# Unequal column parts of 280 and 296 in the dense blocks of a hybrid decoder step, laid side by side over a PSUM bank border

## What is computed

```python
def swiglu(x, w_gu, w_down):
    g, u = jnp.split(x @ w_gu, 2, axis=-1)
    return (jax.nn.silu(g) * u) @ w_down

def trunk_layer(x, ...):
    h = x + 0.5 * swiglu(rms_norm(x, w['g_ffn1']), w['w_ffn1_gu'], w['w_ffn1_down'])
    u = rms_norm(h, w['g_mix'])
    q, k, v, zg, r, us5 = jnp.split(u @ w['w_in'], SPLIT_POINTS, axis=-1)
    ...
    h = h + mix.astype(x.dtype) @ w['w_out']
    h = h + cross_attend(rms_norm(h, w['g_cross']), mem_k, mem_v, w['w_cq'], w['w_co'])
    h = h + 0.5 * swiglu(rms_norm(h, w['g_ffn2']), w['w_ffn2_gu'], w['w_ffn2_down'])
    return h, s_gla, s5_re, s5_im
```

## Time and profile before

| what | value |
|---|---|
| median of three runs | 1283.65 us (1283.48 to 1283.89) |
| profiled execution, its own time | 1281.76 us |
| its span in the profile | 1280.0 us |
| PE busy | 1261.9 us (99% of the span), 10151 matmuls |
| PEld busy | 1218.5 us (95%), 10151 weight loads |
| DVE busy | 856.9 us (67%) |
| ACT busy | 530.4 us (41%) |
| POOL busy | 354.3 us (28%) |
| granted PE clock, mean | 0.996 of full speed |

### The profile page before, as it was taken

How to read it: one execution, slowest core, us unless ns; L and a number is a source line. 1 busy time by engine, 2 the same in 40 slices (tenths; PEclk the granted TensorE clock), 3 DMA queues, 4 the chain that set the end, 5 groups by cost and what they waited for, 6 DMA issues and landing times.

```text
span 1280.0 us, 24086 instructions
## 1 busy us (share of the span) xinstructions
PE 1261.9 (99%) x10151; PEld 1218.5 (95%) x10151; DVE 856.9 (67%) x1061; ACT 530.4 (41%) x803; POOL 354.3 (28%) x411
## 2 busy tenths in 40 slices
PE   7999999999999999999999999999999999999998
PEld 6999999999999999999899997599999999999997
DVE  4986479847985636558565437479995589637953
ACT  6543145511224422574443324246553255414543
POOL 0026623388893201000002100032330133102321
PEclk9999999999999999999999999999999999999998
DMA  6223223263223432125333656322332323323321
GB/s 193 83 83 100 83 84 99 83 136 91 78 66 89 93 79 66 51 69 155 118 91 91 234 199 222 121 83 66 100 100 83 99 83 100 92 82 91 87 63 75
DMA packets 221084, 129.94 MB, mean 102 GB/s; under 512 B 22256, under 2 KB 213280, under 8 KB 220960
## 3 DMA queue, kind: packets, MB, share of 16 engines
q1 hardware_dynamic: 217024, 123.83, 33.1%
q10 hardware_dynamic: 3952, 4.58, 1.1%
HBM read 121.42 MB, written 5.78 MB: 99 GB/s over the span
## 4 chain that ended last, share of the span: by engine, by line
PE 91%; DVE 5%; ACT 2%; issue 1%; DMA 1%; SPq 0%; DVEq 0%; ACTq 0%
PE PS L738 87%; PE PS L1363 1%; DMA AR<-in_x_prompt 1%; DVE xl L2141 1%; DVE ARr L2136 0%; PE PS L808 0%; ACT wh L1502 0%; ACT gua L1651 0%; DVE Hs L2454 0%; PE PS L1449 0%; DVE PS L2120 0%; DVE PS L2130 0%; DVE PS L2123 0%; PE PS L1340 0%; DVE AR L2782 0%
## 5 line engine op out<-in xcount | busy, mean ns | idle before, releaser
L1502 ACT ACTIVATE wh<-raw 128x1024 fp32r<-128x1024 f32 (+1 forms) x126 | 130.1, 1032 | 374.1 <-PE PS L738 374.1
L738 PE MATMUL PS<-yh,wh 128*128 128x288 f32 x960 | 206.1, 296 | 0.0
L738 PE MATMUL PS<-yh,wl 128*128 128x288 f32 x960 | 205.0, 295 | 0.0
L738 PE MATMUL PS<-yl,wh 128*128 128x288 f32 x960 | 205.0, 295 | 0.0
L2029 DVE TENSOR_TENSOR wl<-raw,wh 128x1024 fp32r<-128x1024 f32 (+1 forms) x126 | 154.9, 1229 | 62.3 <-ACT wh L1502 60.9
L738 PE MATMUL PS<-xh,ARr 128*128 128x288 f32 x792 | 173.0, 295 | 0.5 <-ACT sq L1585 0.4
L738 PE MATMUL PS<-xh,wh 128*128 128x288 f32 x736 | 164.2, 305 | 0.1
L738 PE MATMUL PS<-xh,wl 128*128 128x288 f32 x736 | 157.9, 296 | 0.0
L738 PE MATMUL PS<-xl,wh 128*128 128x288 f32 x736 | 157.6, 296 | 0.0
L738 PEld LDWEIGHTS PS<-yh,wh 128*128 128x128 f32 x960 | 154.1, 188 | 1.7 <-DVE yl L2707 0.8
L738 PEld LDWEIGHTS PS<-yl,wh 128*128 128x128 f32 x960 | 154.3, 188 | 0.0
(11 more groups left out here) (378 smaller groups left out, 2206.2 us busy)
## 6 DMA issues: line engine op xcount, KB each, us to landing
raw<-in_w_ffn_gu SPq DMA_DIRECT2D x88, 512.0 KB, 3.7
raw<-in_w_ffn_down SPq DMA_DIRECT2D x32, 512.0 KB, 3.8
raw<-in_w_in SPq DMA_DIRECT2D x16, 512.0 KB, 3.8
raw<-in_w_ckv SPq DMA_DIRECT2D x16, 512.0 KB, 3.7
raw<-in_w_ffn_down SPq DMA_DIRECT2D x16, 384.0 KB, 3.3
Hs<-in_cache_mem_k SPq DMA_DIRECT2D x6, 1024.0 KB, 6.5
raw<-in_w_out SPq DMA_DIRECT2D x8, 512.0 KB, 4.0
raw<-in_w_cq SPq DMA_DIRECT2D x8, 512.0 KB, 4.4
```

The lines of the kernel that those rows point to most:

```text
L738: return e.matmul(out, lhsT, rhs, start=start, stop=stop, **kw)
L1502: e.activation(wh[:, n % 2, 0:K * P], raw[:, n % 4, 0:K * P], ACT.Copy).then_inc(w_hi, 1)
```

## The change

The 576 columns of a dense block are cut at column 280 (`TA`) instead of 288. The first part, 280 columns, goes to the end of the first bank (columns 232 to 511), the second part, 296 columns, to the beginning of the next (columns 0 to 295). The two parts then lie side by side in PSUM, and the eviction reads them as one stretch of 576 columns, `tokens(b)`, where it read two rows of 288. Its other operands lose the `two()`. Each dense matmul pair keeps its weights, its place in the order and its number; the sum of its columns is 576 as before. `mix_part` gets the same parts. The memory key blocks keep their single part of 256 columns. The `unit` products, their halves of 288 columns and their evictions (`halves` at L2208, `two` at L2170) stay, and so does `gate_rank` with L2432. No instruction is added, removed or moved on any engine; 2544 pairs of matmuls and the evictions have other shapes.

The diff, without the evictions at L2393, L2532, L2643 and L2752, which change as L2097 and L2247 do:

```diff
@@ constants @@
 TH = T // 2
+TA = 280
@@ PE, dense @@
-            def dense(n, par, K, xa, xb, width=TH, parts=2, ready=None, inside=None, each=None, ahead=False):
+            PARTS = ((0, TA, 512 - TA), (TA, T, 512))
+            MEMORY = ((0, M, 0),)
+
+            def dense(n, par, K, xa, xb, parts=PARTS, ready=None, inside=None, each=None, ahead=False):
...
                     for wi, (w, x) in enumerate(((wh, xa), (wh, xb), (wl, xa))):
-                        for j in range(parts):
-                            last = mm(bank(b0 + j, width), w[:, par, k * P:(k + 1) * P],
-                                      x[:, k, j * width:(j + 1) * width],
+                        for t0, t1, at in parts:
+                            last = mm(bank(b0, t1 - t0, at=at), w[:, par, k * P:(k + 1) * P], x[:, k, t0:t1],
                                       start=(i == 0 and wi == 0), stop=(i == K - 1 and wi == 2))
@@ PE, memory keys @@
-                    dense(n0 + i, i % 2, KD, mh, ml, width=M, parts=1, ready=(S("memx_lo"), 0) if i == 0 else None)
+                    dense(n0 + i, i % 2, KD, mh, ml, parts=MEMORY, ready=(S("memx_lo"), 0) if i == 0 else None)
@@ PE, mix_part @@
-                        for j in range(2):
-                            last = mm(bank(2 * b + j, TH), w[:, b, k * P:(k + 1) * P], x[:, k, j * TH:(j + 1) * TH],
+                        for t0, t1, at in PARTS:
+                            last = mm(bank(2 * b, t1 - t0, at=at), w[:, b, k * P:(k + 1) * P], x[:, k, t0:t1],
                                       start=(i == 0 and wi == 0), stop=(i == KD - 1 and wi == 2))
@@ DVE @@
+            def tokens(b):
+                return bank(b, T, at=512 - TA)
+
             def halves(b):
                 return PS[:, b:b + 2, 0:TH]
...
-                    STT(two(hk), halves(2 * par), 0.5 if g["half"] else 1.0, two(hk), ALU.mult, ALU.add).then_inc(ps_free, 1)
+                    STT(hk, tokens(2 * par), 0.5 if g["half"] else 1.0, hk, ALU.mult, ALU.add).then_inc(ps_free, 1)
...
-                    TTT(two(gs[:]), halves(6 if n == 2 else 0), two(R[:]), ALU.mult).then_inc(g_scaled, 1)
+                    TTT(gs[:], tokens(6 if n == 2 else 0), R[:], ALU.mult).then_inc(g_scaled, 1)
...
-                    TTT(two(us[:]), halves(2), two(R[:]), ALU.mult).then_inc(ps_free, 1)
+                    TTT(us[:], tokens(2), R[:], ALU.mult).then_inc(ps_free, 1)
...
-                    STT(two(h[:, b, :]), halves(2 * (b % 2)), 0.5, two(h[:, b, :]), ALU.mult, ALU.add).then_inc(ps_free, 1)
+                    STT(h[:, b, :], tokens(2 * (b % 2)), 0.5, h[:, b, :], ALU.mult, ALU.add).then_inc(ps_free, 1)
```

More of the change, by code:

```diff
@@ L2392, in body @@
                     f = i * 2 + (f0 + par)
-                    TTT(two(chunk(PR, f)), halves(2 * par), two(R[:]), ALU.mult).then_inc(ps_free, 1)
+                    TTT(chunk(PR, f), tokens(2 * par), R[:], ALU.mult).then_inc(ps_free, 1)
                 return body
@@ L2531, in _ @@
                 e.wait_ge(mm_done, seq(n) + 3)
-                TTT(two(PR[:, b, :]), halves(2 * (b % 2)), two(R[:]), ALU.mult).then_inc(ps_free, 1)
+                TTT(PR[:, b, :], tokens(2 * (b % 2)), R[:], ALU.mult).then_inc(ps_free, 1)
                 if b:
@@ L2632, in _ @@
                     e.wait_ge(ps_free, seq(n) + 2)
-                STT(two(h[:, i, :]), halves(2 * (n % 2)), 1.0, two(h[:, i, :]), ALU.mult, ALU.add).then_inc(ps_free, 1)
+                STT(h[:, i, :], tokens(2 * (n % 2)), 1.0, h[:, i, :], ALU.mult, ALU.add).then_inc(ps_free, 1)
                 conv(n + 2)
@@ L2751, in _ @@
                 e.wait_ge(mm_done, seq(n) + 3)
-                STT(two(h[:, k, :]), halves(2 * (k % 2)), 1.0, two(h[:, k, :]), ALU.mult, ALU.add).then_inc(ps_free, 1)
+                STT(h[:, k, :], tokens(2 * (k % 2)), 1.0, h[:, k, :], ALU.mult, ALU.add).then_inc(ps_free, 1)
                 conv(n + 2)
```

## The result

The change makes the kernel faster: 1273.32 us (median of 4 runs, 1273.04 to 1275.46) against 1283.77 us for the kernel before beside it. The ratio is 0.9918 with a 95% interval of 0.9906 to 0.9930, so 10.5 us or 0.8%. The profiled execution took 1273.04 us with a span of 1271.2 us; that of the kernel before took 1281.76 and 1280.0.

A forecast was written before the change was run, and what follows sets the result against it. PE's distances between matmuls were taken as the bound. The dense matmuls' -11.0 us, other terms 0, took 1281.76 to 1270.8 us profiled; the median lies 1.9 us above, so 1272.7 us, range 1263 to 1298 us.

The forecast's parts named there:

- What bounds the kernel: PE bounds the kernel: busy 1261.9 of 1280.0 us, 91% of the chain; time is the distances between matmuls.
- The evictions at nothing: 110 DVE evictions read one stretch instead of two rows: at most 1.0 us saved, hidden by the next block; term 0.
- The dense matmuls at 130.9 ns, 11.0 us in all: Dense blocks on PE: 4704 matmuls fall from 133.3 to 130.9 ns, 384 cheap ones lose 0.9 ns each; term -11.0 us.
- An alternation of two lengths breaks a pattern that needs equal ones: Dense pairs: 280 and 296 columns in turn can't repeat the 133.3 ns pattern, so a cheaper one, 130.9 ns, was taken.
- Entered with a certain phase and then kept for the whole stretch: Dense blocks: weight loads and matmuls fall into a regular pattern, kept throughout a stretch, explaining three speeds, 130.0 to 133.3 ns.
- Rival 1: Dense pairs: distance is columns plus a constant, so any cut costs 266.6 ns; 1283.65 or 1285 us; chance 0.17.
- Rival 2: Dense pairs slower because columns move in units of 16: 1302 us, or 1293 us in a milder form; chance 0.27 together.
- The half-size products at nothing: 2772 half-size matmuls keep their code and run near 131.8 ns; term 0, with -5.0 to +4.2 us possible.
- The windows: The five dense 40 us windows of PE's profile should hold 305 to 310 matmuls instead of 302.
- The upper end of the forecast's own range, 1279 us: Slowest outcome of the cheaper-pattern case: dense matmuls at 131.8 ns and the cheap group lost, 1279 us.
- PE's waits as they were: PE's waits for other engines, 16.8 us over 57 places for its weight loads, should stay unchanged.

The follow-up runs named there:

- e1: Changed kernel with equal parts of 288 and 288, still side by side and evicted as one stretch: 1283.34 us, ratio 1.0001 against the kernel before.
- e4: Changed kernel with even blocks cut 288 and 288, odd blocks 280 and 296, all side by side: 1277.95 us, ratio 0.9960 against the kernel before.

## Why the prediction was right, and where it was not

- **What bounds the kernel**: right. PE's chain was it, and the gain is PE busy time, 10.2 us of it ahead of the last steps.
- **The evictions at nothing**: right, 754 to 757 ns after against 752 to 757 before, and e1 measures the edit without the cut as 1.0001.
- **The dense matmuls at 130.9 ns, 11.0 us in all**: right in the sum. The mean is 130.6 ns, and PE's busy time up to the last steps fell by 10.2 us. The way there was not: I took the middle between two cheaper patterns, and the change mixes the cheapest (four fifths of the matmuls) with the dearest. No stretch with 280 ran at 131.7 ns; stretches with 272 and 284 did. That the mix came out at my middle is luck.
- **"An alternation of two lengths breaks a pattern that needs equal ones"**: this step failed. The cuts at 256, 276 and 296 alternate two lengths and run at 133.3 ns throughout, and equal parts ran at 130.0 in one stretch of e1. What the change has is a cut that can hold a cheap pattern, and which cuts can was found only by measuring them. Had it cut at 276, this prediction would have named the same 1272.7 us and been 12 us off.
- **"Entered with a certain phase and then kept for the whole stretch"**: half right. 280 and 288 each have two patterns, and an unbroken stretch keeps the one it has, over up to 1054 matmuls. But e4 shows that the cut decides which patterns there are, and that a block leaves a pattern that its cut can't hold within a few pairs.
- **Rival 1, a straight line**: its 266.6 ns a pair is what 256, 276 and 296 measure, and no cut measured more. For 264, 272, 280 and 284 it is too high. The rule of the Trainium skill whose form it has ("TensorE: Matmul & The Clock Gate", section "Back-to-back issue gap") has no term for where the columns are cut: one sum of columns at the full clock cost 260 to 267 ns a pair here.
- **Rival 2, units of 16 columns**: no cut of eight was dearer than the straight line, multiple of 16 or not. There is no such price.
- **The half-size products at nothing**: right. Over their stretches the mean distance is 131.9 ns before and after.
- **The windows**: four of five were at 310, inside the 305 to 310 that I gave, and the one at 830 us stayed at 302. The two distances of a pair are some 10 ns apart and not 7.
- **The upper end of the forecast's own range, 1279 us**: 1 us too high for its terms, which give 1283.65 - 7.1 (4704 matmuls at 131.8 ns) + 1.3 (the cheap group lost) = 1278 us.
- **PE's waits as they were**: nearly. Ahead of the last steps 1.4 us came back as idle time, in several places of which DVE's `wl` is the largest new one (0.7 us at 384 us). The sum had no term for it, and its term for the matmuls was 0.8 us too large. Together this is why the profiled execution took 1273.04 us where I had 1270.8. The median came within 1 us of the forecast partly by luck: the kernel before was profiled 1.9 us under its median and the changed one only 0.3 us.

What stays open is the cause of the patterns. The means 130.0, 131.7 and 133.3 ns come back in kernel after kernel, but behind one mean stand different patterns: 133.3 ns is a series of four distances with equal parts, of two with 256 + 320 (118 and 149 ns), and of six, the length of one round over the three products, with 276 + 300 and with 296 + 280. In a stretch of these two the dearest distance stays with one of the three products, but it is not the same product in every stretch, so it isn't a product that is dear. The likeliest reading is that weight loads and matmuls fall against each other in a repeating way and that the column at which `x` is cut bears on it; no run shows it. Neither the border's remainder by 16 nor the difference of the lengths orders the eight cuts. Whether it is the address in SBUF or another thing that goes with the border was not taken apart. It could be tried by moving `x` as a whole while the parts stay.

## What to carry to other kernels

Where PE is the bound, take the distance from start to start of its matmuls by stretch, and look for the same shape at two speeds at the full clock: this may be time to be had without any change to the work. Then measure a few cuts of the columns a few columns apart, since four columns decided 0.9% here (276 against 280) and neither a size rule nor the mean duration of an instruction told which. Take several profiles of each, because a single one shows a mix of patterns that partly changes from execution to execution.

## What the runs showed of the hardware

- The fp32r matmul of 288 columns with its own weight load, at the full granted clock, ran at a mean distance of 133.3 or 130.0 ns in dense blocks and of 131.9 ns in half-size products. DMA was busy for the same share (0.27) in a dear and in a cheap window of the kernel before.
- The distances repeat: from the 25th of a stretch on, each is within 2 ns of the one 12 places before it, in the kernel before, with the change and with 256, 264, 272, 276, 284 and 296. The series is 131, 131, 132, 140 ns in a dear stretch of equal parts, 128, 132 in a cheap one, 118, 149 with 256 + 320, and a series of six with 276 + 300 and with 296 + 280.
- 256 + 320, 276 + 300 and 296 + 280 never left 133.3 ns in one profiled execution each, 272 + 304 ran at 131.7 ns but for its first stretch, and 264 + 312 ran at 130.0 ns for over 90% of its matmuls in two executions.
- Moving the cut of 576 columns by 4 (276 to 280) took 11 us off 1284; moving it by 8 from the middle the other way (288 to 296) left it at 133.3 ns throughout.
- Within a pair the two distances are not 7 ns apart, as the columns alone would have it. In the cheap stretches of the changed kernel they are 124.7 ns after the 280 columns and 135.3 ns after the 296, in its dear ones 128.5 and 138.1 ns. At 0.417 ns a column 116.7 and 123.3 ns are columns, so more stands beyond the columns behind the long part than behind the short one.
- A read of 576 columns out of PSUM over a bank border costs DVE 754 to 757 ns, about the same as two rows of 288 (752 to 757 ns); two instructions of 280 and 296 cost 449 + 456 ns.
- PE's last 22 matmuls (20 of them transposes) kept it busy for 4.2 us where the granted clock fell to half among them, and for 2.8 us where it fell behind them. The time from there to the end of the kernel was 10.6 us both times.
